# A hybrid attention layer: two gate blocks moved into the common flow, attention units spaced wider

## The reference

```
h = rmsnorm(x)                       # x: 2048 tokens x 2048, float32
proj = h @ w_in                      # 5376 columns: q_a k_a v_a g_a b c x g_c q_m g_m
o_a = sliding-window attention       # 16 heads of 64, chunks of 64 queries, 128 keys, sinks, bias
o_c = b * causal_conv3(c * x_c)      # 512 channels
o_m = cross-attention to 256 memory tokens   # 4 heads of 128
mixed = concat(silu(g_a)*o_a, silu(g_c)*o_c, silu(g_m)*o_m)
out = x + mixed @ w_out
```

## Time and profile before

| | |
|---|---|
| median of 3 runs | 2934.55 us (2932.59 to 2936.57) |
| the profiled execution's span | 2932.4 us |
| PE busy | 2798.4 us, 95% |
| DVE busy | 1715.3 us, 58% |
| POOL busy | 1291.3 us, 44% |
| ACT busy | 1014.0 us, 35% |

### The profile page before, as it was taken

The page is one execution under the profiler, slowest core; times in us unless marked ns, Lnnn a source line. Parts: engine busy times, 40 slices in busy tenths (PEclk is TensorE's granted clock), DMA queues, the critical chain, the costliest instruction groups (busy, mean ns, idle before and its releaser), DMA issues.

```text
span 2932.4 us, 38165 instructions
## 1 busy us (share of the span) xinstructions
PE 2798.4 (95%) x12859; PEld 2290.5 (78%) x12859; DVE 1715.3 (58%) x3859; ACT 1014.0 (35%) x2125; POOL 1291.3 (44%) x552
## 2 busy tenths in 40 slices
PE   6999999999999999899999998999999999999999
PEld 5887777788887878688888777778888877777887
DVE  5267787433528778814544868762543677874335
ACT  6322424333322333423332332433332223243333
POOL 4545433344454543344445453334444454333444
PEclk9999999999999999999999999999999999999999
DMA  6332222245532223234543222223453322222344
GB/s 210 111 92 73 80 86 72 87 128 164 167 94 74 84 72 94 65 100 150 162 139 94 72 82 78 79 83 110 152 176 111 89 77 80 80 79 86 122 165 143
DMA packets 160522, 312.65 MB, mean 107 GB/s; under 512 B 11558, under 2 KB 21876, under 8 KB 157556
## 3 DMA queue, kind: packets, MB, share of 16 engines
q1 hardware_dynamic: 139348, 258.30, 29.4%
q10 hardware_dynamic: 21024, 52.44, 5.5%
HBM read 293.13 MB, written 17.56 MB: 106 GB/s over the span
## 4 chain that ended last, share of the span: by engine, by line
issue 59%; POOL 38%; PE 1%; SPq 1%; POOLq 1%; DMA 0%; DVE 0%; ACT 0%; ACTq 0%
POOL w_lo L414 35%; POOL q_scale L420 2%; POOL early L428 1%; SPq L346 1%; POOLq L413 0%; DMA raw<-in_w_mem_kv 0%; POOL x_scale L420 0%; PE acc L1129 0%; PE acc L1131 0%; PE acc L1130 0%; POOL k_scale L420 0%; ACT w_hi L482 0%; SPq L348 0%; PE ps_t L1182 0%; POOLq L459 0%
## 5 line engine op out<-in xcount | busy, mean ns | idle before, releaser
L414 POOL TENSOR_TENSOR w_lo<-raw,w_hi 128x1024 fp32r<-128x1024 f32 x482 | 1181.6, 2452 | 1608.4 <-ACT w_hi L482 1608.3
L482 ACT ACTIVATE w_hi<-raw 128x1024 fp32r<-128x1024 f32 x482 | 509.9, 1058 | 1244.0 <-PE acc L1131 1228.9
L1129 PE MATMUL acc<-h_hi,w_hi 128*128 128x512 f32 x1792 | 717.4, 400 | 35.5 <-DVE stage L983 15.2
L1130 PE MATMUL acc<-h_lo,w_hi 128*128 128x512 f32 x1792 | 708.6, 395 | 0.0
L1131 PE MATMUL acc<-h_hi,w_lo 128*128 128x512 f32 x1792 | 707.6, 395 | 0.0
L937 DVE STREAM_TRANSPOSE probs_t<-probs 32x128 f32<-32x128 f32 x1536 | 465.2, 303 | 27.9 <-PE ps_o L1223 5.6
L1129 PE MATMUL acc<-w_hi,mix_hi 128*128 128x512 f32 x1088 | 428.0, 393 | 16.9 <-DVE stage L1114 9.4
L1129 PEld LDWEIGHTS acc<-h_hi,w_hi 128*128 128x128 f32 x1792 | 343.2, 192 | 118.3 <-DVE stage L983 16.3
L1130 PE MATMUL acc<-w_lo,mix_hi 128*128 128x512 f32 x1088 | 424.8, 390 | 0.0
L1131 PE MATMUL acc<-w_hi,mix_lo 128*128 128x512 f32 x1088 | 424.7, 390 | 0.0
L1131 PEld LDWEIGHTS acc<-h_hi,w_lo 128*128 128x128 f32 x1792 | 342.9, 191 | 73.7
(11 more groups left out here) (150 smaller groups left out, 2342.5 us busy)
## 6 DMA issues: line engine op xcount, KB each, us to landing
raw<-in_w_in SPq DMA_DIRECT2D x336, 512.0 KB, 3.6
raw<-in_w_out SPq DMA_DIRECT2D x130, 512.0 KB, 3.8
xt<-in_x ACTq DMA_DIRECT2D x16, 1024.0 KB, 6.3
stage<-in_x ACTq DMA_DIRECT2D x64, 256.0 KB, 5.5
out<-stage ACTq DMA_DIRECT2D x64, 256.0 KB, 2.9
raw<-in_w_mem_kv SPq DMA_DIRECT2D x16, 512.0 KB, 7.5
ungated<-in_x SPq DMA_DIRECT2D x2, 1024.0 KB, 13.0
early<-in_x SPq DMA_DIRECT2D x2, 1024.0 KB, 11.1
```

Source lines behind the costliest of these rows:

```text
L414: nc.gpsimd.tensor_tensor(w_lo[:, slot_mod % 2, :], raw[:, slot_mod, :], w_hi[:, slot_mod % 2, :].bitcast(F32), ALU.subtract).then_inc(lo_ ...
L482: nc.scalar.activation(w_hi[:, slot_mod % 2, :], raw[:, slot_mod, :], ACT.Copy).then_inc(hi_ready, 1)
L1129: nc.tensor.matmul(dst, st[0], mv[0], start=first, stop=False)
L1130: nc.tensor.matmul(dst, st[0], mv[1], start=False, stop=False)
```

## The change

The blocks GA0 and GA1 join the list BLOCKS, at its end, so that their slots 68 to 83 are part of the written-out flow on all engines and the loops over LAST_GATES go. What is computed, the order of the blocks, the loads, and the count of slots are the same; where a count of blocks stood in a semaphore's target, it is adapted. Then the tables of the units change. Scores of units 0 to 7 go to slots 16, 17, 19, 20, 22, 23, 25, 26, those of units 8 to 23 to slots 29, 32, ..., 74. Transposes, splits and values follow by the same distances, so the last values are in slot 77. Scaling, turning, means, conv blocks and evacuations keep their slots.

```diff
-BLOCKS = ["KV", "QM", "QA0", "QA1", "C", "X", "B", "GM", "GC"]
+BLOCKS = ["KV", "QM", "QA0", "QA1", "C", "X", "B", "GM", "GC", "GA0", "GA1"]
...
-GATED = {"GM": (0, 3), "GC": (1, 2)}
-LAST_GATES = 2
...
+GATED = {"GM": (0, 3, 8), "GC": (1, 2, 0), "GA0": (2, 0, 16), "GA1": (3, 1, 24)}
+GATES0 = len(BLOCKS) - len(GATED)
 FLOW_SLOTS = KV_SLOTS + SB_SLOTS * (len(BLOCKS) - 1)
...
-SCORES_AT = {FLOW0 + 4 + u: u for u in range(8)}
-SCORES_AT.update({FLOW0 + 17 + 2 * u: 8 + u for u in range(8)})
-SCORES_AT.update({FLOW0 + min(39 + 2 * u, 52): 16 + u for u in range(8)})
+SCORES_AT = {FLOW0 + 4 + 3 * u // 2: u for u in range(8)}
+SCORES_AT.update({FLOW0 + 17 + 3 * u: 8 + u for u in range(16)})
...
-                with act.Fori(0, LAST_GATES) as n:
-                    for s in range(SB_SLOTS):
-                        if s == SB_SLOTS - 1:
-                            gate_tanh(g, n + 2, base + GATE_SLOT0 + n * SB_SLOTS + SB_SLOTS)
-                        high((s + 2) % 4, base + GATE_SLOT0 + n * SB_SLOTS + s + 2)
-                        if s == SB_SLOTS - 1:
-                            gate_high(g, n + 2, n)
...
-                    gate(g, *GATED[name], 8 if name == "GM" else 0)
+                    gate(g, *GATED[name])
...
-                with dve.Fori(0, LAST_GATES) as n:
-                    gate(g, n + 2, n, UNITS)
...
-                with pe.Fori(0, LAST_GATES) as n:
-                    for s in range(SB_SLOTS):
-                        feature_slot(s, s % 2, base + GATE_SLOT0 + n * SB_SLOTS + s,
-                                     g * USES + n + MEM_USES + len(BLOCKS))
```

More of the change, by code:

```diff
@@ L48 @@
 TOKEN_BLOCKS = ("KV", "QM", "QA0", "QA1")
-BLOCKS = ["KV", "QM", "QA0", "QA1", "C", "X", "B", "GM", "GC"]
+BLOCKS = ["KV", "QM", "QA0", "QA1", "C", "X", "B", "GM", "GC", "GA0", "GA1"]
 COLUMN = {"KV": KV_A, "QM": Q_M, "QA0": Q_A, "QA1": Q_A + 512, "C": C_C, "X": X_C, "B": B_C,
-          "GM": G_M, "GC": G_C}
-GATED = {"GM": (0, 3), "GC": (1, 2)}
-LAST_GATES = 2
+          "GM": G_M, "GC": G_C, "GA0": G_A, "GA1": G_A + 512}
+GATED = {"GM": (0, 3, 8), "GC": (1, 2, 0), "GA0": (2, 0, 16), "GA1": (3, 1, 24)}
+GATES0 = len(BLOCKS) - len(GATED)
 FLOW_SLOTS = KV_SLOTS + SB_SLOTS * (len(BLOCKS) - 1)
-GATE_SLOT0 = FLOW_SLOTS
-OUT_SLOT0 = GATE_SLOT0 + LAST_GATES * SB_SLOTS
+OUT_SLOT0 = FLOW_SLOTS
 GROUP_SLOTS = OUT_SLOT0 + 4 * SB_SLOTS
@@ L60 @@
 OUT_PAIRS = (0, 1, 4, 5, 6, 7, 2, 3)
-USES = len(BLOCKS) + LAST_GATES + 4
+USES = len(BLOCKS) + 4
 MEM_USES = 2
@@ L455, in _ @@
                               q_rstd)
-                with pool.Fori(0, LAST_GATES) as n:
-                    for s in range(SB_SLOTS):
-                        low((s + 2) % 4, base + GATE_SLOT0 + n * SB_SLOTS + s + 2)
                 with pool.Fori(0, 4) as n:
@@ L566, in gate_tanh @@
                 for b in range(4):
-                    sums_stand(act, g * DONE + m * 3 + MEM_DONE + 3 * (len(BLOCKS) - 2), b, slots)
+                    sums_stand(act, g * DONE + m * 3 + MEM_DONE + 3 * GATES0, b, slots)
                     act.wait_ge(mix_lo_ready, g * 16 + m * 4 + 1)
@@ L664, in _ @@
                     if s in LAST_SLOT and LAST_SLOT[s][1] in GATED:
-                        gate_high(g, *GATED[LAST_SLOT[s][1]])
+                        gate_high(g, *GATED[LAST_SLOT[s][1]][:2])
                     if s in VALUES_AT:
@@ L701, in _ @@
                             for t in range(TT):
-                                act.wait_ge(bank_free[t], g * USES + n + MEM_USES + len(BLOCKS) + LAST_GATES + 1)
+                                act.wait_ge(bank_free[t], g * USES + n + MEM_USES + len(BLOCKS) + 1)
                                 act.dma_start(out[bass.ds(g * TOK + t * P, P), bass.ds(n * 512, 512)],
@@ L988, in gate @@
                 for b in range(4):
-                    dve.wait_ge(bank_free[b], g * USES + m + MEM_USES + len(BLOCKS) - 1)
+                    dve.wait_ge(bank_free[b], g * USES + m + MEM_USES + GATES0 + 1)
                     nc.vector.scalar_tensor_tensor(
@@ L1111, in _ @@
                         dve.wait_ge(resid_in, g * 256 + n * 64 + 64)
-                        sums_stand(dve, g * DONE + n * 3 + MEM_DONE + 3 * (len(BLOCKS) + LAST_GATES),
+                        sums_stand(dve, g * DONE + n * 3 + MEM_DONE + 3 * len(BLOCKS),
                                    t, base + OUT_SLOT0 + n * SB_SLOTS + SB_SLOTS)
@@ L1301, in _ @@
                         token_slot(s, SB_SLOTS, s % 2, base + OUT_SLOT0 + n * SB_SLOTS + s,
-                                   g * USES + n + MEM_USES + len(BLOCKS) + LAST_GATES, mix_hi, mix_lo, TT,
+                                   g * USES + n + MEM_USES + len(BLOCKS), mix_hi, mix_lo, TT,
                                    OUT_PAIRS[s])
```

4 lines of the change are left out of this document (removed).

## The result

| | before | after |
|---|---|---|
| median | 2934.96 us (4 runs, 2932.59 to 2936.57) | 3002.21 us (4 runs, 2998.80 to 3006.66) |
| ratio, 95% interval | | 1.0230 (1.0216 to 1.0245) |
| the profiled execution's span | 2932.4 us | 2997.0 us |
| slots 16 to 83, mean of the four groups | 441.0 us | 457.4 us |

The changed kernel is 2.3% slower: 67 us by the medians, 64.6 by the spans. The mean of slots 16 to 83 grew by 16.4 us, which is 65.6 in four groups; slots 0 to 15 and the output slots 84 to 115 are as before within 0.3 a group.

What follows compares the result with a forecast made beforehand. PE is busy 95% and loses time only in waits, where DVE is late. Predicted losses of 52.1 us against 35.5 give +16.6 per group, +66; 2932.4 + 66 + 2.1 = 3000.5 us, range 2948 to 3026 (about 8 in 10).

Steps and rivals of the forecast that it cites:

- (1): Slots 16 to 28: 1.0 us wait in slot 16 for turned queries; slot 28 6.8 late, turning ahead of unit 7.
- (2): X at slot 43: its first bank waits for DVE to end unit 12's transposes, 1.2 us.
- (3): Slots 44 to 52: DVE's fixed-order work of 53.8 us against PE's 40.7, plus 7.8 of w_lo meetings: 20.9 us.
- (4): GM at slot 59: gate starts on time but delays softmax 18, so w_lo for slot 62 is 4.4 us late.
- (5): GC at slot 67: 1.2 us for the first bank, 3.3 for unit 20's low half behind the gate.
- (6): GA0 at slot 75: 1.6 us before slot 76, 4.3 in slot 77 for unit 23's low half behind the gate.
- (7): Small hand-overs, 0.6 us per group.
- (8): Clock falls after waits over 3.2 us, in slots 28, 47 to 52, 62 and 77: four at 1.7, 6.8 us.
- Faster: Rival: DVE gets the port first wherever both want it and w_lo waits: -2.2 us per group, 2926; chance 0.10.
- No meetings: Rival: DVE meets no w_lo at the shared port: +3.5 us per group, 2948.5; no meetings or few, chance 0.17.
- Late for good: Rival: DVE stays late from slot 52 on, waits in every scores slot: +14 us per group, 3055; given little chance.

Runs made afterwards that it cites:

- The third experiment: Changed kernel with the second and third step of each conv block run over 8 of 512 tokens: 2988.22 us, ratio 1.0175.
- the last three runs: Changed kernel with units 14 and 15 out of slots 44 to 52 (2944.27 us); with its own table (2828.18); that table with unit 13's scores at 49 (2827.86).

## Why the prediction was right

3000.5 us were predicted, 3002.21 measured; +16.6 per group predicted, +16.4 measured. A total can agree by luck, so here is each step, in us per group, with group 2 of the changed kernel. "Measured" is the slot's time less its own work, which is taken from an equal slot that waits for nothing (5.44 empty, 6.63 with values and scores, 6.03 with values alone).

| step | predicted | measured | from |
|---|---|---|---|
| (1) slot 16 | 1.0 | 1.0 | slot 16 7.39 |
| (1) before slot 28 | 6.8 | 6.4 | slot 27 12.06, own 5.68 |
| (2) X | 1.2 | 1.3 | slot 43 6.70 |
| (3) slots 45 to 51 | 20.9 | 20.7 | 61.4 less 40.7 |
| (4) GM | 4.4 | 4.2 | slot 61 9.64 |
| (5) GC | 4.5 | 4.3 | slots 67 and 68 6.70, 9.69 |
| (6) GA0 | 5.9 | 5.5 | slots 75 and 77 7.07, 9.87 |
| (7) hand-overs | 0.6 | 0.7 | the remainder |
| (8) clock | 6.8 | 6.2 | slots 28, 52, 62 |
| sum | 52.1 | 50.3 | 455.76 less 405.5 |

Groups 2 and 3 lost 50.3, group 0 51.7 and group 1 55.4; their mean is 51.9. Group 1's surplus is in single slots. Slot 51 took 11.52 in place of 9.35, as one 128x4 step of the edges met a w_lo there, a meeting that step (3) had not counted:

```profile
1156.33 2.32 DVE L954 TENSOR_TENSOR edge<-vecs,carry 128x4 f32<-128x4 f32 x1
...
1156.29 2.34 POOL L408 TENSOR_TENSOR w_lo<-raw,w_hi 128x1024 fp32r<-128x1024 f32 x1 [10.52 <-ACT w_hi L473]
```

Slot 69 (7.20 in place of 5.58, granted clock 0.76) and slots 77 and 78 (1.4 more together, 0.93 and 0.85) are falls of the clock that group 2 doesn't have. Groups 2 and 3 lost 1.8 less than the 52.1 predicted; that the mean of the four came so near it is partly luck, as the other meetings and falls of groups 0 and 1 made up for it.

Step (1) in the trace: DVE's order was read rightly, turning ahead of unit 7's softmax.

```profile
1709.98 7.15 DVE L845 STREAM_TRANSPOSE early<-ungated 32x256 f32<-32x256 f32 x16
1717.16 0.69 DVE L873 TENSOR_REDUCE shift<-ps_s 128x2 f32<-128x512 f32 x1
```

Slot 28 started at 1719.45, 6.2 late on ACT's evacuation. The size was right. That the order was the reason was not: with the order turned round the lateness stayed.

Step (3) in the trace, which carried two fifths of the sum. DVE did the operations in the order listed. It was never idle between softmax 13 and the first bank of B but for the exponentials inside each softmax and one gap of 0.22. PE's slot 52 started at 1885.94, 0.75 behind the start of B's evacuation, 61.4 after the end of slot 44. The sum of single durations was 53.8, and the meetings add 7.5 here:

```profile
1843.23 2.01 DVE L852 TENSOR_TENSOR pt_lo<-probs_t,pt_hi 128x512 fp32r<-128x512 f32 x1
...
1858.09 2.63 DVE L936 TENSOR_SCALAR ungated<-early,vecs 128x512 f32<-128x512 f32 x1
1860.75 2.77 DVE L937 SCALAR_TENSOR_TENSOR ungated<-early,vecs,ungated 128x511 f32<-128x511 f32 x1
...
1871.52 2.71 DVE L852 TENSOR_TENSOR pt_lo<-probs_t,pt_hi 128x512 fp32r<-128x512 f32 x1
...
1885.19 2.48 DVE L1001 TENSOR_TENSOR ungated<-acc,ungated 128x512 f32<-128x512 f32 x4
```

The two low halves were held 1.3 and 2.0, as predicted (1.3 and 1.9). Elsewhere I had put the low half at 0.7, as if it met nothing, and all 64 took 2.05 in the mean; in the stretches that have slack this cost PE nothing (slots 30 to 43 took 82.86 with X's 1.3 as their only wait), so the bill of DVE was short by 1.4 a unit without harm to the sum. Conv block 0 was mis-sized: two of its steps met a w_lo, 2.1 and 2.0, 4.2 in place of 2.3. Conv block 3 met none, where 2.3 was predicted. 7.5 against 7.8, then, with two errors that cancel. The third experiment shows how easily they might not have: a shift of a few tenths adds and removes meetings of 2 us each.

The clock, step (8): the granted clock reads 0.75 in slot 28 and 0.71 in slot 62, behind waits of 6.2 and 4.0 us, and 0.76 in slot 52; part of the matmuls of these slots ran at 1.2 GHz, the others at 2.4. It reads 1.00 in slot 77 with a wait of 3.7, where a fourth fall was counted; in groups 0 and 1 that fall came, in groups 2 and 3 it didn't. The three that came cost 2.0, 2.6 and 1.6 where 1.7 each was put: in this group the number was high, the price low. Nor is 3.2 us of waiting, from which step (8) counts, a border: in group 2 of the kernel before the clock fell in slot 24 (0.80) behind a wait of 2.7 in slot 23. What decides a fall, no run here shows.

The rivals. "Faster" fell: the port didn't go to DVE wherever both wanted it. Where w_lo started first, by a few hundredths as at 1858.06 and 1858.09, DVE was held. Where DVE started first, w_lo waited, as beside the scaling of group 2, which took its 2.29 while w_lo took 4.41 in place of 2.4:

```profile
1699.76 2.29 DVE L826 TENSOR_TENSOR ungated<-ungated,q_scale 128x2048 f32<-128x2048 f32 x1 [1.91 <-POOL q_scale L414]
...
1699.91 4.41 POOL L408 TENSOR_TENSOR w_lo<-raw,w_hi 128x1024 fp32r<-128x1024 f32 x1 [0.18 <-ACT w_hi L473]
```

Of the 64 low halves 52 started behind a w_lo and were held. Four more followed straight on the last step of a gate that had made w_lo wait already, and weren't held: 0.68, while w_lo took 3.04. "No meetings" fell too, with meetings at four places in slots 44 to 52 (2.01, 2.63, 2.77, 2.71). "Late for good" fell: slots 53 to 60 have no wait. (Its price was added up wrong by 2: 14 us more per group give 3057, not 3055.) The condition of being wrong, slots 44 to 52 under 60 us, is met only by kernels with other tables of units (53.05 with the old one, 57.57, 57.89 and 58.10 with those of the last three runs).

The experiments on single edits went worse than the prediction of the whole. For the turning at slot 40 I had priced the slots that would be relieved and had not added up those that would carry it, as step (3) had done. For the turning behind unit 7 the stretch was added up and came out, and a fall of the clock behind the moved wait had been put at nothing.

## What to carry to other kernels

Where an engine has a fixed order and long pieces of work, add up its operations between two points at which another engine needs it, and compare with that engine's own work between them; spacing one kind of work evenly, with the other kinds left where they are, makes some stretches overfull. Moving one piece within an overfull stretch, or out of it into a gap shorter than the piece, only moved the wait here (3001 and 3002 us): take whole units out (75.4 to 57.6 us here), or make a table in which each long piece stands in a gap of its own (2934 to 2828 us). Slack counts only where it lies in one piece that is as long as the work that is to go there.

## What the hardware showed that was not expected

The holding of DVE isn't bound to large operations nor to two large inputs. Held by a w_lo of 2.4 us were a TENSOR_SCALAR from one SBUF tensor and a column of vecs (2.63 in place of 0.49), a step over 8 columns (2.25 in place of 0.23), a step over 4 columns (2.32 in place of 0.15) and the eight small h_lo steps (3.14 in place of 2.31). Not held were the transposes of 32x128: sixteen of them at 1794.26 took 5.05, as in the earlier trace rows, while w_lo ran from 1794.78 to 1797.18, and the sixteen of 32x256 at 1836.04 took 7.16 while w_lo ran from 1836.86 to 1839.26.
By the Trainium skill (SBUF — State Buffer, "SBUF: two separate sides") the lock concerns a DVE operation in a two-port mode or one with two SBUF inputs, against a GpSimd operation that reads SBUF. The trace agrees for the steps with two tensors and for the transposes; the TENSOR_SCALAR with a single tensor and a column of vecs was held as well, and no run here tells which of the two conditions it meets.

Two w_lo back to back (4.92 us from 1858.06) let DVE's first step end between them, and held the next one again: one DVE operation was done per w_lo, over 511 columns as over 8 (2.77 and 2.25). The pair took 4.92 where another pair took 4.67 (from 1947.90), so DVE's step cost POOL a quarter of a microsecond in return. It is behind late exponentials that ACT hands POOL two weights at once, so a late softmax can bring two holds in a row.

The low half is held by construction in the quiet slots. There ACT writes the high half right behind w_hi, so POOL's w_lo and DVE's low half become ready within half a microsecond of each other, and w_lo is first: 1800.16 against 1800.63, and the low half takes 2.47 in place of 0.69.
